# Two transformer blocks on one core: key, value, logit and first projections moved into the query pipeline, the other projections staggered, gate projections placed beside the second block's early attention

## What is computed

```python
# first block, each layer
h = rms(x) * g
qa, ka, va, qd, kd, vd, beta, decay, z, gates = split(h @ w_in)
y_attn = attention(rope(rms(qa)), rope(rms(ka)), va) @ w_o_attn      # 8 heads, 512 x 512
qd, kd, vd = silu(conv5(qd, kd, vd)); qd, kd = l2norm(qd), l2norm(kd)
o = delta_rule(qd, kd, vd, sigmoid(beta), -exp(a) * softplus(decay + b))   # both directions
y_dn = (rms(o) * silu(z)) @ w_o_dn
x += (sigmoid(gates0) * y_attn + sigmoid(gates1) * y_dn) @ w_out
x += (silu(conv3(h2 @ w_up)[0]) * conv3(h2 @ w_up)[1]) @ w_down
# second block, each layer
h = rms(x) * g
o_a = nsa(q, k, v, compressed keys and values, 24 gates)             # three causal attentions, added
o_f = forgetting_attention(fq, fk, fv, forget logits)
o_m = attention over 256 memory rows
x += sum(sigmoid(g_i) * ((o_i * silu(s_i)) @ w_i)) @ w_out
```

## Time and profile before

| | us |
|---|---|
| median of three runs | 3871.32 |
| lowest, highest | 3870.57, 3876.25 |
| the profiled execution | 3863.87 |
| its span in the trace | 3862.1 |
| mean granted clock of PE | 0.941 |

### The profile page before, as it was taken

How to read it: one execution, slowest core, us unless ns; L and a number is a source line. 1 busy time by engine, 2 the same in 40 slices (tenths; PEclk the granted TensorE clock), 3 DMA queues, 4 the chain that set the end, 5 groups by cost and what they waited for, 6 DMA issues and landing times.

```text
span 3862.1 us, 61717 instructions
## 1 busy us (share of the span) xinstructions
PE 3447.8 (89%) x26780; PEld 2707.1 (70%) x26780; DVE 1891.2 (49%) x2840; ACT 1578.4 (41%) x2640; POOL 214.5 (6%) x204
## 2 busy tenths in 40 slices
PE   7687899999996888989999987899899878999989
PEld 4476777778874676867788855676677656776777
DVE  5455544565564555544755643432434544434333
ACT  6533224433255433233433455445423545363432
POOL 0022220000000132300000000000000000000000
PEclk9898899999998898999999997999999988999999
DMA  3000013322230000023223221121122211121212
GB/s 136 22 8 24 24 35 96 102 93 93 97 101 33 12 19 29 14 86 100 94 93 99 73 89 60 34 72 55 55 74 75 99 36 58 50 69 52 63 63 93
DMA packets 74926, 249.11 MB, mean 65 GB/s; under 512 B 9248, under 2 KB 10912, under 8 KB 73376
## 3 DMA queue, kind: packets, MB, share of 16 engines
q1 hardware_dynamic: 74656, 245.16, 19.4%
HBM read 237.82 MB, written 6.29 MB: 63 GB/s over the span
## 4 chain that ended last, share of the span: by engine, by line
PE 76%; DVE 10%; ACT 9%; issue 3%; POOL 1%; DMA 1%; SPq 0%; ACTq 0%; DVEq 0%; POOLq 0%
PE psum L463 73%; ACT s_tmp L1154 3%; PE psum L634 2%; ACT L1154 2%; DVE s_xb L1742 1%; DVE s_tmp L1745 1%; ACT s_w L1154 1%; DVE s_nm L1824 1%; DVE s_tmp L1742 1%; DVE s_ffy L1745 1%; DVE s_w L1742 1%; PE psum L548 1%; DMA s_stage<-woa 1%; ACT s_h L1154 0%; DVE psum L1742 0%
## 5 line engine op out<-in xcount | busy, mean ns | idle before, releaser
L463 PE MATMUL psum<-s_h,s_w 128*128 128x512 f32 (+1 forms) x6864 | 1656.4, 399 | 28.8 <-DVE s_w L1742 19.7
L463 PEld LDWEIGHTS psum<-s_h,s_w 128*128 128x128 f32 (+1 forms) x6864 | 1296.6, 191 | 330.3 <-issue 29.7
L1742 DVE TENSOR_TENSOR s_w<-s_stage,s_w 128x1024 fp32r<-128x1024 f32 (+2 forms) x468 | 521.5, 1116 | 685.6 <-ACT s_w L1154 684.3
L1154 ACT ACTIVATE s_w<-s_stage 128x1024 fp32r<-128x1024 f32 (+2 forms) x468 | 451.2, 966 | 336.1 <-PE psum L463 303.4
L463 PE MATMUL psum<-s_ffa,s_w 128*128 128x512 f32 x1056 | 249.0, 396 | 3.8 <-DVE s_ffa L1742 3.8
L1154 ACT ACTIVATE s_E<-psum,s_nm 128x256 f32<-128x256 f32 (+3 forms) x224 | 115.7, 518 | 333.5 <-DVE s_nm L1824 190.5
L1154 ACT ACTIVATE s_tmp<-psum 128x512 f32<-128x512 f32 (+5 forms) x194 | 110.5, 572 | 343.3 <-PE psum L463 334.2
L1154 ACT ACT_TABLE_LOAD x185 | 237.4, 1283 | 8.1 <-DMA s_x<-xT 4.8
L463 PE MATMUL psum<-s_oR,s_w 128*128 128x512 f32 (+1 forms) x960 | 229.3, 391 | 8.2 <-DVE s_oR L1742 8.2
L463 PEld LDWEIGHTS psum<-s_ffa,s_w 128*128 128x128 f32 x1056 | 197.5, 187 | 54.2 <-DVE s_ffa L1742 6.4
L463 PE MATMUL psum<-s_tmp,s_cst 128*128 128x512 f32 (+2 forms) x236 | 134.2, 680 | 107.2 <-ACT s_tmp L1154 107.2
(11 more groups left out here) (244 smaller groups left out, 3588.2 us busy)
## 6 DMA issues: line engine op xcount, KB each, us to landing
s_stage<-w SPq DMA_DIRECT2D x192, 512.0 KB, 3.3
s_stage<-wup SPq DMA_DIRECT2D x88, 512.0 KB, 3.3
s_stage<-wo SPq DMA_DIRECT2D x32, 512.0 KB, 3.3
s_stage<-wdn SPq DMA_DIRECT2D x32, 512.0 KB, 3.6
s_stage<-wdn SPq DMA_DIRECT2D x16, 384.0 KB, 3.2
spill<-s_x SPq DMA_DIRECT2D x2, 2048.0 KB, 8.2
s_stage<-woa SPq DMA_DIRECT2D x16, 256.0 KB, 2.6
s_x<-spill SPq DMA_DIRECT2D x2, 2048.0 KB, 8.6
```

What stands on the lines that cost most here:

```text
L463: return self.e.matmul(out, left, right, start=first, stop=last, skip_group_check=True)
L1154: return self.e.activation(out, src, func, **kw)
L1742: return self.e.tensor_tensor(out, a, b, op)
```

## The change

In both blocks the query pipeline has eight projections instead of six or four. In the first block the two new ones are `bd` and the first projection of the delta rule; in the second they are k0, v0, k1, v1, and `projected` is gone. There the normalised input is made four chunks a turn. In `mixed` the second projection lane starts two steps late while the first has done two already, so they are four steps apart; the small activations of `scalars` are grouped by function, and its cumulative sums stand later in steps. `lanes` sets memory, then (hidden, then compressed) and the gates, one in three steps, abreast of each other, one step for each unit of attention; `compressed` has buffers of its own (vc, cE, cPT, cR), E2 has four buffers instead of three, and `norm` of the memory uses cPT. In the first input's preparation the squares follow the copies. A smaller scratch for dynamic DMAs makes room.

```diff
-    def mixed(self, l, attention, scalars, project, gates):
+    def mixed(self, l, attention, scalars, begun, project, gates):
...
-        beside(abreast(scalars(), project(0, (0,)), project(0, (1,))), fill, 1, 1)
+        beside(abreast(scalars, begun, delayed(project(0, (1,)), 2)), fill, 1, 1)
...
-def lanes(first, attentions, second, memory, hidden, compressed, *gates):
-
-    rest = itertools.chain(second, abreast(memory, hidden), compressed, *gates)
-    beside(first, rest, 1, 1)
-    beside(paced(itertools.chain(*attentions), 2, 1), rest, 5, 6)
+def lanes(attentions, memory, hidden, compressed, *gates):
+
+    rest = abreast(memory, itertools.chain(hidden, compressed), spread(itertools.chain(*gates), 3))
+    beside(paced(itertools.chain(*attentions), 2, 1), rest, 1, 1)
     for _ in rest:
         pass
+
+
+def delayed(steps, n):
+    for _ in range(n):
+        yield
+    yield from steps
...
-        self.bE, self.bPT = sb("E2", [128, 3, T]), sb("PT2", [128, 2, T])
+        self.bE, self.bPT = sb("E2", [128, 4, T]), sb("PT2", [128, 2, T])
...
-        self.vc = self.sg[:, 0, 0:256].rearrange("p (a n) -> p a n", a=2)
-        self.cE, self.cPT, self.cR = (self.sg[:, i, :] for i in (1, 2, 3))
+        self.vc, self.cE, self.cPT, self.cR = sb("vc", [128, 2, 128]), sb("cE", [128, T]), sb("cPT", [128, T]), sb("cR", [128, T])
...
+        scalars, begun = self.scalars(l, hi, lo, ht), self.project(l, 0, (0,), hi, lo, ht)
+
         def first(c):
-            self.lin((l, "q", c) if c < 5 else (l, "v"), wt[l, c], 8, m.raw[:, 0], m.raw[:, 1], raw, amid=(lambda: self.total(tag)) if c == 0 else None)
+            if c < 6:
+                self.lin((l, "q", c) if c < 5 else (l, "v"), wt[l, c], 8, m.raw[:, 0], m.raw[:, 1], raw, amid=(lambda: self.total(tag)) if c == 0 else None)
+            elif c == 6:
+                next(scalars)
+            else:
+                next(begun)
+                next(begun)
...
-        for _ in behind(first, rest, 6, 2):
+        for _ in behind(first, rest, 8, 2):
...
         def first(c):
-            if c:
+            if c in (1, 2, 3):
                 self.lin((L, "q", c), wt[l, c], 8, rhi, rlo, raw)
+            elif c > 3:
+                self.lin(kv(c), wt[l, 2 + c], 8, hi, lo, ht)
...
-        together(self.forgetting(l, rhi, rlo, raw), behind(first, lambda c: self.qk((L, "q", c), K_BO, K_PB), 4, 2))
+        together(self.forgetting(l, rhi, rlo, raw), behind(first, rest, 8, 2))
...
+            if tag != "in":
+                square(c)
+            yield
+        if tag == "in":
+            for c in range(8):
+                square(c)
...
-        uppers = self.uppers(("two", l), hi)
+        uppers = self.uppers(("two", l), hi, 4)
...
-    nc = _bacc.Bacc("TRN2", target_bir_lowering=False, num_devices=1)
+    nc = _bacc.Bacc("TRN2", target_bir_lowering=False, num_devices=1, dynamic_dma_scratch_size=4096)
```

More of the change, by code:

```diff
@@ L764, in scalars @@
         self.give((key, "T"), ("vec_dn", key, "bd1"))
-        yield
-        yield
-        yield
+        for _ in range(6):
+            yield
         ps = self.take((key, "cum"))
@@ L1001, in layer2 @@
         self.w.wait_ge(*self.at("vec_set", "sel"))
-        kv = lambda b: self.projected(l, b, hi, lo, ht)
-        lanes(kv(0), [self.attention(L, nsa_attn(m, l, b), "gated") for b in range(2)], kv(1), self.memory(l),
+        lanes([self.attention(L, nsa_attn(m, l, b), "gated") for b in range(2)], self.memory(l),
               self.hidden(l, hi, lo, ht), self.compressed(l), silu_gate(0, 10), merge_gates())
@@ L1079, in hidden @@
             yield
+            self.k.marks[key] = self.used
             yield
@@ L1756, in raw @@
         n, col, made = self.raws(tag)
-        if c > 1:
+        if c > 1 and tag != "in":
             self.total(tag, c - 1)
@@ L1864, in run @@
                 self.one_ahead()
+        for c in range(1, 7):
+            self.total("in", c)
         self.w.wait_ge(*self.at("dma_rope", 0))
@@ L1879, in layer1 @@
         normal = self.normal(tag)
+        scalars, begun = self.scalars(l), self.project(l, 0, (0,))
+        keys = [(l, "q", c) for c in range(5)] + [(l, "v"), (l, "bd"), (l, "p", 0, 0, 0)]
         def rest(c):
-            self.scaled_in_place((l, "q", c) if c < 5 else (l, "v"), tag)
-            next(normal, None)
+            if c < 6:
+                self.scaled_in_place(keys[c], tag)
+                next(normal, None)
             if c < 5:
                 self.qk((l, "q", c), m.aq[:, c, :] if c < 4 else m.ak[:, :], 0.125 if c < 4 else 1.0, True)
-        for _ in behind(lambda c: self.ahead((l, "q", c) if c < 5 else (l, "v")), rest, 6, 2):
+            elif c == 6:
+                next(scalars)
+            elif c == 7:
+                next(begun)
+                next(begun)
+        for _ in behind(lambda c: self.ahead(keys[c]), rest, 8, 2):
             pass
@@ L2161, in layer2 @@
         normal = self.normal(("two", l))
+        keys = [(L, "q", c) for c in range(4)] + [(L, n, b) for b in range(2) for n in "kv"]
         def rest(c):
-            self.scaled_in_place((L, "q", c), ("two", l))
-            next(normal, None)
-            self.qk((L, "q", c), m.bq[:, c, :], 0.125, True)
-        together(self.forgetting(l), behind(lambda c: self.ahead((L, "q", c)), rest, 4, 2))
+            if c < 4:
+                self.scaled_in_place(keys[c], ("two", l))
+                next(normal, None)
+                next(normal, None)
+                self.qk(keys[c], m.bq[:, c, :], 0.125, True)
+            elif c % 2 == 0:
+                self.qk(keys[c], m.bk[:, c // 2 - 2, :], 1.0, True)
+        together(self.forgetting(l), behind(lambda c: self.ahead(keys[c]), rest, 8, 2))
         g24 = m.g24
```

103 lines of the change are left out of this document (48 added, 55 removed).

## The result

The changed kernel takes **3772.16 us** (median of four runs, 3764.29 to 3778.53); the kernel before, measured with it, 3873.78. The ratio is 0.9737, with a 95% interval of 0.9715 to 0.9758. The forecast was 3769, its range 3730 to 3840. The profiled execution of the changed kernel took 3773.13 us, its span is 3771.3, that is 90.8 less than that of before.

What follows compares the result with a forecast made beforehand. PE, busy 3447.8 of 3862.1 us, bounds the kernel; time leaves through fewer waits or fuller clock. First block 64, second 43, less 4.4, gave 102.6: 3863.9 to 3761.3, plus 7.4 is 3769 us, range 3730 to 3840.

Steps and rivals of the forecast that it cites:

- Moved projections: First block, query pipeline's end: gate logits and first projection fill PE's waits for ACT; 11.5 us per layer.
- Wait for the decay logits: First block, before the cumulative sums: earlier chain and more PE work cut the 10.84 us wait; gain 7.5 per layer.
- Staggering: First block: projection lanes four turns apart stop waits coming in pairs; 9 of 22.9 us per layer, bounds 0 and 18.
- Clock, 4: First block, granted clock 0.83: a quarter of 16 us comes back, 4 us per layer, bounds 0 and 16.
- Start and tail: Squares after copies at kernel's start lose 1.4 us; uncovered last attention turns lose 1.5 per layer; together -4.4.
- Query pipeline of the second block: Three of four key and value projections fill PE's waits between queries; 3.5 us per layer, bounds -3 and 12.
- Gates beside the early attention: Second block: twelve gate projections, moved earlier, fill a third of waits (11 us per layer) and raise the clock (7).
- The median, +7.4: Whole kernel: the runs' median, 3871.3 us, is 7.4 above the profiled execution, so 7.4 is added to the sum.
- Rival B: Only direct moves pay; waits move with the attention's chain, the second block gains nothing: 3838 us, chance 0.18.
- no change: Whole kernel: the time stays the same, about 0.2% or 8 us being the least a measurement can tell; chance 0.04.
- Rival C: Both blocks: half of all low-clock time goes, each microsecond costing half; 50 us against 22, so 3741 us, chance 0.17.
- Rival D: Second block's early attention: gates' activations hold up exponentials in ACT's queue; slower, up to 3942 us, chance 0.04.

Runs made afterwards that it cites:

- experiment 10: Changed kernel with six projections again in the first block's query pipeline, logits and first projection after it, lanes four steps apart: 3782.91 us.
- experiment 11: Changed kernel with the logits' small activations in the old order and the cumulative sums after three steps instead of six: 3765.34 us.
- experiment 8: Kernel before, with only the first block's second projection lane delayed by four steps: 3841.74 us.
- (7): Changed kernel with the first block's two projection lanes running level instead of four steps apart: 3786.63 us.
- experiment 12: Changed kernel with each square behind its copy again at the kernel's start, DVE adding squares between the chunks: 3773.18 us.
- (6): Changed kernel with the gates late again and SP issuing one more weight tile ahead of the compressed key/value copies: 3753.57 us, ratio to before 0.9692.
- experiment 2: Kernel before with only the fourth E2 buffer and the smaller DMA scratch making room: 3825.88 us, ratio to before 0.9881.
- experiments 4 and 5: Changed kernel with the tile first (SP issues one more weight tile ahead of compressed key/value copies), run twice: 3739.00 and 3743.79; then median 3750.01 us.
- experiments 3: Changed kernel with the second block's gates late again, early-attention fill one after the other: 3750.52 us, ratio to before 0.9687.

## Why the prediction came out right, and what in it was wrong

The time was met to 3 us, and that is luck: by the traces the first block and the start gave 47 us where 59.6 were forecast, the early attention lost 17.6 (some 7 without the luck of before's trace) instead of giving 36, and a buffer without a term gave 53.6. By its own steps:

- **Moved projections, 11.5 per layer.** The waits of the earlier trace rows are filled, as said. Net it is 5.4 and 3.9 (experiment 10): the term did not count what B gives back.
- **Wait for the decay logits, 7.5.** The wait of 10.84 is gone, all of it; but undoing the later place costs only 2.8 and 0.3 (experiment 11). PE waits at the next step instead. The term counted one wait and not what is late next.
- **Staggering, 9.** The mechanism is right, the size too small: 15.8 and 16.9 alone (experiment 8), 13.7 and 10.4 when undone (7). The three terms overlap: the first block gave 24.0 and 23.9 us per layer in A and B together, not 28 + 4.
- **Clock, 4.** In layer 1 of A 6.3 us of busy time went, at 0.92 for 0.86.
- **Start and tail, -4.4.** -1.1 at the first sum of squares, of which 0.4 reaches the units (experiment 12); nothing at the tail, B is unchanged.
- **Query pipeline of the second block, 3.5.** 4.2 and 5.5: right in kind, some 2 us small in layer 1, which repeats.
- **Gates beside the early attention, 11 idle and 7 clock per layer.** Wrong in sign: F grew by 5.0 in layer 0 and, against the 354 of most executions, by some 2 in layer 1. Two steps failed. One is "SP issues the gates' tiles earlier; DMA is busy 0.18 of the time at most there, so it hides": the transfer's share of time was not the point, its place in SP's queue was, and that cost 10.4 us in layer 1. The other is the third taken of the waits and of the low clock: without the stall (6) the early gates give 3.2 us in layer 1, not 18, since 20.7 of the 42.9 us of waits in F are for ACT s_tmp, inside a step where a norm follows its own projection. The prediction had said so of "many of those waits" and then taken a third of all.
- **The fourth E2 buffer, no term at all.** It is named in the change, and was worth 53.6 us by G and H, 47 by the medians of experiment 2. The profile had shown it: in G and H of layer 0 PE was idle 15.5 and 11.6 us before (the two rows of experiment 2), with waits for DVE s_PT and DVE s_w in its timeline. The prediction's windows ended at 2566 in layer 0 and 3379 in layer 1 and took what follows as untouched.
- **The median, +7.4.** It was right to forecast the median rather than the one execution; the likely reason for the distance is F of layer 1 at 0.93.

Rival B (only direct moves) and no change are out by the time, though B's account of the early attention, that the waits move with it and nothing is gained, is close to what F showed. Rival C (the clock gives back more) is out where most of its extra was to come from: F kept 0.89 in layer 0, and the whole kernel went from 0.941 to 0.945. In the first block it had a point: by the two rows of A in layer 1 the time at the low clock fell from about 55 to 28 us, half as C said, but 6.3 us of busy time went with it and not half of 27. Rival D had the right stretch and the wrong queue: a gate's entry in an in-order queue did hold up the exponentials, once per layer and not at each gate, and through its weight tile, not its own activation.

Of the signs listed: logits and first projection between the last sums, yes; no wait of 10.8, yes; units 30 us earlier, 22.8; busy over 80%, 84% of A in layer 0 and 83% in layer 1; clock near 0.88, 0.93 and 0.92 over A; attention 36 us shorter in two layers, no; PE waits of about 22 us in each, no.

On the price of low clock: F of layer 1 with and without the stall has 313.33 and 307.39 us of busy time at 0.89 and 0.91, that is 78 and 62 us at half speed:

```profile
3031.80:3377.70 345.90, 307.39 (x1826) 232.90 (x1825) 134.30 (x247) 171.63 (x338) 0.00 (x0) 0.91 0.16 53
```

5.9 us for 16, or 0.37 per microsecond, as the prediction had from its two stretches (the clocks have two digits, which leaves room for 0.26 to 0.65). The 91 entries behind the stall, worked out in the same way, give 6.3 for 14, or 0.45, and F of layer 0 in the two traces of experiments 4 and 5 (rows in the last section) 12.0 for 22, or 0.54. The Trainium skill, page "TensorE: Matmul & The Clock Gate", section "Terms", gives 1 - K/N, here 0.5; the runs lie on both sides of it, mostly below, and do not exclude it.

The changed kernel with the tile first has the lowest median, 0.968 of before. The two with late gates (experiments 3 and 6) are not told apart from it by their intervals.

## What to carry to other kernels

Give every edit of a diff its term, a buffer count too: ask which instruction waits for the buffer, and what stands behind it in its engine's queue. When a projection is moved, follow its weight tile through the issuing queue as well as the matmuls through PE's; here a copy that waited for data held up the prefetch behind it, with the DMA engines busy only 0.16 of the time. And count waits that are filled together with the stretch behind them: three terms of 11.5, 7.5 and 9 us, and 4 for the clock, were 24 together.

## What had not been expected of the hardware

One wait of PE of 5.15 us was followed by 16 us at a granted clock of 0.56, where the same work without it ran at 1.00 in 10.2, and it cost 10.4 us in all. And the same instructions scatter with the clock: F of layer 0 took 337.2 and 348.5 us in two executions of one kernel,

```profile
2255.60:2592.80 337.20, 298.01 (x1827) 225.61 (x1826) 134.38 (x247) 171.43 (x339) 0.00 (x0) 0.94 0.16 55
2257.80:2606.40 348.60, 310.01 (x1827) 234.50 (x1826) 134.30 (x247) 171.97 (x339) 0.00 (x0) 0.91 0.16 53
```

and 350.0 to 359.0 in others with the changed kernel's F, while F of layer 1 stayed within 0.3 us for each of the two. That is no rule for layer 1: with the order of before it took 343.8 us once and 353.9 and 354.0 elsewhere. A difference of under 10 us in a kernel of 3800 is therefore better read from a stretch that repeats than from the total of one execution.
